# Router matmuls of two output stages with the router stationary and the tokens moving

## The chip, the cores and the metric

One core of a Trainium2 chip runs the whole kernel. The metric is the device time of one execution in microseconds, lower is better.

## What is computed

Two transformer blocks run one after the other on 1024 tokens of width 1024, in float32. Each block ends its mixer with an output projection and then sends the normed tokens to a mixture of experts, and it is the router in between that the change touches. Cut to that, the reference is:

```python
# first block, after the short-convolution mixer has given y
lat = lat + g1 * (y @ w_out)                        # output projection and residual
h = modulate(rms_norm(lat, norm_g), sh2, sc2)
aff = softmax(h @ w_router)                         # 16 router columns
g, idx = top_k(aff.T, 128)                          # each expert takes its best 128 tokens
# second block, after the mLSTM and pooling mixer
x = x + gate_a * (mix @ w_out)
h = rms_norm(x, norm2_g) * (1 + scale_f) + shift_f
g_logits = h @ w_rg + b_rg                          # 4 router columns
e_logits = h @ w_re + b_re                          # 32 more; kept together as 36 columns
# best group, best two experts in it, tokens sorted into blocks by expert
```

## The kernel before, in words

The program is written by hand, engine by engine. Each engine runs its own list of instructions in order, and the engines meet only at counting semaphores. Matrices are split into a high and a low part (type fp32r), and each product is made of three fp32r matmuls (helper `three`, L1719 to L1727); transposes and the router run in plain float32.

An **output stage** stands at the end of each block's mixer: `output_stage` exists once for each engine and runs twice, first with 16 router columns (`router1`), later with 36 (`router2`). It goes through the 1024 tokens in 8 tiles of 128. For tile t, TensorE multiplies the mixer's output with `w_out` into two PSUM banks (L1796 to L1806: eight chunks, two column halves, three fp32r matmuls each, 48 matmuls of 512 columns). VectorE then multiplies by the gate (L1268), adds the residual (L1271), ScalarE squares and sums (L893), VectorE and GpSimd make the inverse root (L1273, L634), and VectorE scales and shifts (L1276, L1279) into the one buffer `h2t`. GpSimd sends `h2t` to DRAM (L638), TensorE transposes it in eight pieces (L1788), ScalarE copies the transposed tile to `h2T` (L888), and TensorE multiplies it with the router (L1813).

The software pipeline is written out by hand. In step s, TensorE runs the projection of tile s, puts the eight transposes of tile s-1 in before chunk 6 of 8 (L1797), and the router of tile s-1 after chunk 8. The last step (s = 8) has no projection: transposes, then the router. ScalarE's step s is: slice and round the next tile of the mixer's output (L873), copy of `h2T` (L888), squares of tile s (L893). VectorE's L1268 writes `h2t` and so waits for three things: the projection of its tile (`y_ready`), the transposes of the tile before (`tr2`) and the landing of the tile before in DRAM (`h2_out`).

The router of a tile is 8 matmuls of depth 128: `h2T[:, k, :]` (128 columns, the tokens) is the stationary operand, `router[:, k, :]` (16 or 36 columns) moves. In the profile each float32 matmul has two records, so 8 matmuls are 16 passes. The logits of all tiles gather in PSUM bank 6, tokens on partitions, and VectorE reads them once at the end, in L1291 (first stage) and L1556 (second).

What follows the first stage on ScalarE: six DMA issues that bring back sums needed much later (L903), and the exponential of the softmax (L905), before which a table of functions is loaded. VectorE then picks the 128 best tokens for each expert in 16 rounds (L1304 to L1309), and everything after hangs on that. After the second stage VectorE works out ranks and slots (L1556 to L1625). SyncE starts to load expert weights into the ring of 12 buffers (L508, L550) as soon as its last residual tile of the stage is asked for.

TensorE, ScalarE and the others run the nine steps by `in_pairs` (L55): three steps written out, a hardware loop over pairs, the rest written out.

```python
                pe.wait_ge(S["h2T_ready" + b], s + past["h2T_ready" + b])
                for k in range(KD):
                    last = pe.matmul(ps[:, 6, bass.ds((s - 1) * width, width)], h2T[:, k, :], router[:, k, :],
                                     start=(k == 0), stop=(k == KD - 1))
                last.then_inc(S["rt_done" + b], 1)
```

Of the kernel before, what the change touches and what calls it, by code (L numbers as in the profile page):

```python
# [12 lines left out]
P = 128  # L13
D = 1024
T = 1024
NT = T // P
# [6 lines left out]
E1 = 16  # L23
# [9 lines left out]
    silu_ready sq_done mod_ready tr_ready tr_hi split_hi f_part cv_done c_copied route1 e1_exp m1_used m1_hi  # L33
    m1_xT m1_xT_hi slots_ready m1_silu m1_hT m1_hT_hi if_hi v_even gate_exp branch d2_out uc_ready cell_in
    q_mm m_mm dmask pm_ready m_out wt_diag wt_rest pv hn_tr num_out final_in dve_steps cols_tr mod_mm xn_done
    tr_lo sums_out sums2_out sums_in row_cols row_tr row_copied rows_out rows_here aff_ready affT_tr m1_xT_lo m1_hid m1_hT_lo if_lo v_odd if_mm gt_ready pool_mm k_mm k_out s_mm
    hn_ready q_out
"""

# [44 lines left out]
def build(nc, ctx, io, out, room):  # L84
# [23 lines left out]
    mod = sb("mod", [P, 2, 48])  # L108
    gain = sb("gain", [P, 4, 8])
    rowsT = sb("rowsT", [32, P])  # L110
    ident = sb("ident", [P, P])
    ones = sb("ones", [P, P])
    neghalf = sb("neghalf", [P, 8])
# [123 lines left out]
    for name in SEMS.split():  # L237
# [11 lines left out]
        [("row_tr", 1), ("row_tr_2", 1)],  # L249
        [("row_copied", 1), ("row_copied_2", 1)],  # L250
        [("rows_out", 16), ("rows_out_2", 16)],
        [("rows_here", 64), ("rows_here_2", 64)],
        [("var_ready", 1), ("var_ready_2", 1), ("hv_ready", 4)],
        [("rstd_ready", 1), ("rstd_ready_2", 1), ("hr_ready", 4)],
# [544 lines left out]
    def _(act):  # L799
# [67 lines left out]
        def output_stage(b):  # L867
            def token_slice(q, r):

                t = 2 * q + r  # L870
                if not (static(q) and t < 2):
                    act.wait_ge(S["y_ready" + b], t - 1 + past["y_ready" + b])
                act.activation(zsH[:, r, :, :], xz[:, :, bass.ds(t * P, P)], ACT.Copy).then_inc(S["zs_hi" + b], 1)  # L873

            token_slice(0, 0)
            for k in range(KD):
                if b == "":
                    split_hi(4, k, woH[:, k, :], (S["f_part"], 3 * KD) if k == 0 else None)
                else:
                    d2_hi(16 + k)  # L880

            def o_step(q, r):
                s = 2 * q + r
                if not (static(q) and s >= NT - 1):
                    token_slice(q, 1) if r == 0 else token_slice(q + 1, 0)
                if not (static(q) and s == 0):
                    act.wait_ge(S["tr2" + b], s + past["tr2" + b])
                    act.activation(h2T[:].rearrange("p (a b) c -> p a (b c)", a=2), ps[:, 4:6, :],  # L888
                                   ACT.Copy).then_inc(S["h2T_ready" + b], 1)
                if not (static(q) and s == NT):  # L890
                    act.wait_ge(S["x1_done" + b], s + 1 + past["x1_done" + b])

                    act.activation(h2t[:], xt[:, r, :], ACT.Square, accum_out=stat[:, 4, 0:1]).then_inc(S["sq2" + b], 1)  # L893

            in_pairs(act, NT + 1, o_step)
# [822 lines left out]
    def _(pe):  # L1718
# [61 lines left out]
        def output_stage(b, router, width):  # L1780
            def o_step(q, r):
                s = 2 * q + r
                first, final = static(q) and s == 0, static(q) and s == NT

                def transposes():
                    pe.wait_ge(S["h2_done" + b], s + past["h2_done" + b])
                    for c in range(KD):
                        last = pe.transpose(ps[:, 4 + c // 4, (c % 4) * P:(c % 4 + 1) * P], h2t[:, c * P:(c + 1) * P],  # L1788
                                            ident[:])
                    last.then_inc(S["tr2" + b], 1)  # L1790

                if not final:
                    pe.wait_ge(S["zs_lo" + b], s + 1 + past["zs_lo" + b])
                    if not (static(q) and s < 2):
                        pe.wait_ge(S["x1_done" + b], s - 1 + past["x1_done" + b])
                    for k in range(KD):  # L1796
                        if k == 6 and not first:  # L1797
                            transposes()
                        if first and b == "":
                            pe.wait_ge(S["split_done"], 3 * KD + k + 1)  # L1800
                        if first and b == "_2":
                            pe.wait_ge(S["d2_split"], 16 + k + 1 + past["d2_split"])
                        last = three([ps[:, 2 * r + n, :] for n in range(2)], zsH[:, r, k, :], zsL[:, r, k, :],
                                     [(woH[:, k, 512 * n:512 * n + 512], woL[:, k, 512 * n:512 * n + 512])
                                      for n in range(2)], k == 0, k == KD - 1)
                    last.then_inc(S["y_ready" + b], 1)  # L1806
                else:
                    transposes()
                if first:
                    return  # L1810
                pe.wait_ge(S["h2T_ready" + b], s + past["h2T_ready" + b])
                for k in range(KD):
                    last = pe.matmul(ps[:, 6, bass.ds((s - 1) * width, width)], h2T[:, k, :], router[:, k, :],  # L1813
                                     start=(k == 0), stop=(k == KD - 1))
                last.then_inc(S["rt_done" + b], 1)

            in_pairs(pe, NT + 1, o_step)

        pe.wait_ge(S["small_in"], 16 * 8)
        pe.wait_ge(S["row_copied"], 1)  # L1820
# [324 lines left out]
```

## Time and profile before

| | us |
|---|---|
| median of three runs | 2603.82 (2603.05 to 2608.44) |
| the profiled execution, its own time | 2599.45 |
| its span in the profile | 2597.8 |
| around the span | 1.65 |
| PE busy in the span | 2137.4 (82%) |
| first output stage, from PE's first projection matmul to the end of its last router matmul | 376.68 to 499.90 |
| second output stage, the same | 1612.57 to 1735.73 |

All times inside the execution are microseconds from the start of the span. PE is TensorE's matmuls and PEld its loads of stationary operands, DVE is VectorE, ACT ScalarE, POOL GpSimd, SP SyncE. A name with q behind it is an engine's instruction sequencer, which issues DMAs without the engine's arithmetic unit. In a row, `128*128 128x16` means a stationary operand of 128 rows by 128 columns and 16 moving columns. What stands in brackets is idle time and what ended it. A matmul's duration has its way through the array in it, so the pace of a run of them is read from start to start, not from durations.

### The profile page before, as it was taken

The numbers are of one execution on the slowest core, as the hardware profiler recorded it, in microseconds if no ns is written. First come the engines' busy times: TensorE is split into PE (matmuls) and PEld (weight loads), VectorE is DVE, ScalarE is ACT, GpSimd is POOL, SyncE is SP. The second block draws the span as 40 slices with busy tenths as digits, with TensorE's granted clock in tenths as the row PEclk, the third lists the DMA queues.
The fourth block names the chain that finished last, engine by engine and source line by source line (L and its number), as shares of the span: only waits on it lengthen the run. The fifth ranks groups of instructions, "written<-read, shape, count | busy, mean of one in ns | idle before, by whom it ended". The sixth has DMA issues, their size and how long they took to land. (4 is left out here: it accounts for less than half of the span.)

```text
span 2597.8 us, 30729 instructions
## 1 busy us (share of the span) xinstructions
PE 2137.4 (82%) x9605; PEld 1711.3 (66%) x9605; DVE 1711.3 (66%) x1868; ACT 1197.7 (46%) x1389; POOL 219.1 (8%) x261
## 2 busy tenths in 40 slices
PE   1899979729999999966989866963999999997850
PEld 1688868728888888855868445853888877775320
DVE  4566654589999999965053345444998989895015
ACT  2211112118777777753031323213888888884011
POOL 0000001000000000000000100103001101000013
PEclk9899989759999999996689977976999999998985
DMA  8077653519999999991010301343999999997645
GB/s 280 12 258 229 230 194 115 210 33 379 383 382 380 388 381 383 382 317 43 17 33 25 134 1 49 111 174 136 392 398 399 398 399 398 399 397 296 240 179 201
DMA packets 282879, 633.45 MB, mean 244 GB/s; under 512 B 24488, under 2 KB 63164, under 8 KB 282812
## 3 DMA queue, kind: packets, MB, share of 16 engines
q1 hardware_dynamic: 245248, 520.16, 54.7%
q0 software_dynamic: 27280, 97.10, 10.7%
q10 hardware_dynamic: 10284, 15.32, 1.7%
q8 instruction: 40, 0.66, 0.1%
q14 instruction: 27, 0.22, 0.0%
HBM read 573.18 MB, written 59.31 MB: 243 GB/s over the span
## 5 line engine op out<-in xcount | busy, mean ns | idle before, releaser
L1644 DVE TENSOR_TENSOR mL<-ring,mH 128x1024 fp32r<-128x1024 f32 x384 | 459.4, 1221 | 49.2 <-ACT mH L1057 40.3
L1324 DVE TENSOR_TENSOR mL<-ring,mH 128x1024 fp32r<-128x1024 f32 x384 | 459.1, 1223 | 33.2 <-ACT mH L911 14.4
L911 ACT ACTIVATE mH<-ring 128x1024 fp32r<-128x1024 f32 x384 | 403.3, 1061 | 95.9 <-PE ps L1726 95.8
L1057 ACT ACTIVATE mH<-ring 128x1024 fp32r<-128x1024 f32 x384 | 401.1, 1058 | 77.4 <-DMA ring<-in_w_expert_gate 30.5
L1723 PE MATMUL ps<-mH,xsH 128*128 128x512 f32 x1024 | 412.6, 403 | 7.3 <-DVE mL L1644 4.3
L1726 PE MATMUL ps<-mH,xsL 128*128 128x512 f32 x1024 | 402.0, 393 | 0.0
L1724 PE MATMUL ps<-mL,xsH 128*128 128x512 f32 x1024 | 401.1, 392 | 0.0
L1723 PEld LDWEIGHTS ps<-mH,xsH 128*128 128x128 f32 x1024 | 193.6, 189 | 46.1 <-issue 7.3
L1726 PEld LDWEIGHTS ps<-mH,xsL 128*128 128x128 f32 x1024 | 193.4, 189 | 43.0
L1724 PEld LDWEIGHTS ps<-mL,xsH 128*128 128x128 f32 x1024 | 193.9, 189 | 37.4
L1723 PE MATMUL ps<-mH,hidH 128*128 128x512 f32 x512 | 201.5, 394 | 3.5 <-DVE mL L1644 3.5
L1724 PE MATMUL ps<-mL,hidH 128*128 128x512 f32 x512 | 200.2, 391 | 0.0
L1726 PE MATMUL ps<-mH,hidL 128*128 128x512 f32 x512 | 158.2, 390 | 0.0
L1723 PE MATMUL ps<-hH,wH 128*128 128x512 f32 x384 | 151.7, 395 | 5.8 <-DVE wL L1183 5.8
L1724 PE MATMUL ps<-hL,wH 128*128 128x512 f32 x384 | 150.7, 392 | 0.0
L1144 DVE SCALAR_TENSOR_TENSOR acc<-ring,silu_c,acc 128x1024 f32<-128x1024 f32 x84 | 107.9, 1284 | 27.6 <-DMA ring<-in_ada_w 21.6
L1726 PE MATMUL ps<-hH,wL 128*128 128x512 f32 x384 | 119.1, 392 | 0.0
L1723 PE MATMUL ps<-woH,zsH 128*128 128x512 f32 x256 | 104.6, 408 | 11.2 <-DVE woL L1401 6.2
L1723 PEld LDWEIGHTS ps<-mH,hidH 128*128 128x128 f32 x512 | 96.5, 188 | 23.4 <-issue 3.7
L1726 PEld LDWEIGHTS ps<-mH,hidL 128*128 128x128 f32 x512 | 96.5, 189 | 20.4
L1724 PEld LDWEIGHTS ps<-mL,hidH 128*128 128x128 f32 x512 | 96.6, 189 | 19.5
L1724 PE MATMUL ps<-woL,zsH 128*128 128x512 f32 x256 | 101.8, 398 | 0.0
(357 smaller groups left out, 3147.2 us busy)
## 6 DMA issues: line engine op xcount, KB each, us to landing
ring<-in_w_expert_gate SPq DMA_DIRECT2D x144, 512.0 KB, 14.9
ring<-in_w_expert_up SPq DMA_DIRECT2D x144, 512.0 KB, 10.8
ring<-in_w_expert_down SPq DMA_DIRECT2D x144, 512.0 KB, 13.6
ring<-in_moe_w_gate SPq DMA_DIRECT2D x128, 512.0 KB, 8.3
ring<-in_moe_w_up SPq DMA_DIRECT2D x128, 512.0 KB, 7.7
ring<-in_moe_w_down SPq DMA_DIRECT2D x128, 512.0 KB, 8.0
ring<-in_ada_w SPq DMA_DIRECT2D x96, 512.0 KB, 5.4
yslot_dram<-xz POOLq DMA_DIRECT2D x32, 512.0 KB, 6.8
```

What stands on the lines that cost most here:

```text
L911: act.activation(mH[:, m % WSETS, :], ring[:, m % RING, :], ACT.Copy).then_inc(S["m1_hi"], 1)
L1057: act.activation(mH[:, wset, :], ring[:, slot, :], ACT.Copy).then_inc(S["m2_hi"], 1)
L1144: ins = dve.scalar_tensor_tensor(out=acc[:], in0=slot, scalar=silu_c[:, silu_col + k:silu_col + k + 1], in1=acc[:], op0=ALU.mult, op1=ALU.add)
L1324: dve.tensor_tensor(mL[:, m % WSETS, :], ring[:, m % RING, :], mH[:, m % WSETS, :].bitcast(F32), ALU.subtract).then_inc(S["m1_lo"], 1)
L1644: dve.tensor_tensor(mL[:, wset, :], ring[:, slot, :], mH[:, wset, :].bitcast(F32), ALU.subtract).then_inc(S["m2_lo"], 1)
L1723: pe.matmul(o, high, rh, start=start, stop=False)
L1724: pe.matmul(o, high, rl, start=False, stop=False)
L1726: last = pe.matmul(o, low, rh, start=False, stop=stop)
```

## The change

The operands of the router swap places: the router's 16 or 36 columns become stationary, and the tile's 128 tokens move. The result has logits on partitions and tokens along columns, in PSUM bank 7. ScalarE copies it to a new small buffer `lgT` in SBUF, and TensorE transposes it back into its place in bank 6, one step later and ahead of the next router, so that VectorE still reads the same layout. In the last step the last tile is transposed back at once. Two semaphores are added, `rl_done` (router matmuls done) and `lgT_copied`. ScalarE's copy stands between the copy of `h2T` and the squares. TensorE's nine steps are written out, without the hardware loop.

```diff
--- before.py
+++ after.py
@@ -33,7 +33,7 @@
     silu_ready sq_done mod_ready tr_ready tr_hi split_hi f_part cv_done c_copied route1 e1_exp m1_used m1_hi
     m1_xT m1_xT_hi slots_ready m1_silu m1_hT m1_hT_hi if_hi v_even gate_exp branch d2_out uc_ready cell_in
     q_mm m_mm dmask pm_ready m_out wt_diag wt_rest pv hn_tr num_out final_in dve_steps cols_tr mod_mm xn_done
-    tr_lo sums_out sums2_out sums_in row_cols row_tr row_copied rows_out rows_here aff_ready affT_tr m1_xT_lo m1_hid m1_hT_lo if_lo v_odd if_mm gt_ready pool_mm k_mm k_out s_mm
+    tr_lo sums_out sums2_out sums_in row_cols row_tr row_copied rows_out rows_here rl_done lgT_copied aff_ready affT_tr m1_xT_lo m1_hid m1_hT_lo if_lo v_odd if_mm gt_ready pool_mm k_mm k_out s_mm
     hn_ready q_out
 """
 
@@ -108,6 +108,7 @@
     mod = sb("mod", [P, 2, 48])
     gain = sb("gain", [P, 4, 8])
     rowsT = sb("rowsT", [32, P])
+    lgT = sb("lgT", [NR2, P])
     ident = sb("ident", [P, P])
     ones = sb("ones", [P, P])
     neghalf = sb("neghalf", [P, 8])
@@ -249,6 +250,8 @@
         [("row_tr", 1), ("row_tr_2", 1)],
         [("row_copied", 1), ("row_copied_2", 1)],
         [("rows_out", 16), ("rows_out_2", 16)],
+        [("rl_done", NT), ("rl_done_2", NT)],
+        [("lgT_copied", NT), ("lgT_copied_2", NT)],
         [("rows_here", 64), ("rows_here_2", 64)],
         [("var_ready", 1), ("var_ready_2", 1), ("hv_ready", 4)],
         [("rstd_ready", 1), ("rstd_ready_2", 1), ("hr_ready", 4)],
@@ -887,6 +890,11 @@
                     act.wait_ge(S["tr2" + b], s + past["tr2" + b])
                     act.activation(h2T[:].rearrange("p (a b) c -> p a (b c)", a=2), ps[:, 4:6, :],
                                    ACT.Copy).then_inc(S["h2T_ready" + b], 1)
+                    act.wait_ge(S["rl_done" + b], s + past["rl_done" + b])
+                    if not (static(q) and s == 1):
+                        act.wait_ge(S["rt_done" + b], s - 1 + past["rt_done" + b])
+                    width = E1 if b == "" else NR2
+                    act.activation(lgT[0:width, :], ps[0:width, 7, 0:P], ACT.Copy).then_inc(S["lgT_copied" + b], 1)
                 if not (static(q) and s == NT):
                     act.wait_ge(S["x1_done" + b], s + 1 + past["x1_done" + b])
 
@@ -1808,13 +1816,23 @@
                     transposes()
                 if first:
                     return
+                def token_logits(back):
+                    pe.wait_ge(S["lgT_copied" + b], s - back + 1 + past["lgT_copied" + b])
+                    pe.transpose(ps[:, 6, bass.ds((s - back) * width, width)], lgT[0:width, :],
+                                 ident[0:width, 0:width]).then_inc(S["rt_done" + b], 1)
+
+                if not (static(q) and s < 2):
+                    token_logits(2)
                 pe.wait_ge(S["h2T_ready" + b], s + past["h2T_ready" + b])
                 for k in range(KD):
-                    last = pe.matmul(ps[:, 6, bass.ds((s - 1) * width, width)], h2T[:, k, :], router[:, k, :],
+                    last = pe.matmul(ps[0:width, 7, 0:P], router[:, k, :], h2T[:, k, :],
                                      start=(k == 0), stop=(k == KD - 1))
-                last.then_inc(S["rt_done" + b], 1)
-
-            in_pairs(pe, NT + 1, o_step)
+                last.then_inc(S["rl_done" + b], 1)
+                if final:
+                    token_logits(1)
+
+            for s in range(NT + 1):
+                o_step(s // 2, s % 2)
 
         pe.wait_ge(S["small_in"], 16 * 8)
         pe.wait_ge(S["row_copied"], 1)
```

## Rows read from the trace of the kernel before

**Rows 1.** The page: busy time of each engine

```profile
PE 2137.4 (82%) x9605; PEld 1711.3 (66%) x9605; DVE 1711.3 (66%) x1868; ACT 1197.7 (46%) x1389; POOL 219.1 (8%) x261
```

**Rows 2.** Busy time by stretches, body and tail, first stage: PE PEld DVE ACT POOL PEclk DMA GB/s

```profile
394.00:484.00 90.00, 90.00 (x475) 76.65 (x474) 40.17 (x39) 19.89 (x27) 11.09 (x20) 1.00 0.50 171
484.00:505.00 21.00, 9.04 (x47) 7.48 (x46) 7.69 (x12) 3.76 (x5) 1.65 (x3) 0.59 0.72 264
```

**Rows 3.** Timeline of VectorE, gate multiply L1268: first stage, then second

```profile
404.57 1.23 DVE L1268 TENSOR_TENSOR h2t<-ps,gate_row 128x1024 f32<-128x1024 f32 x1 [5.90 <-DMA h_dram<-h2t]
...
456.86 1.22 DVE L1268 TENSOR_TENSOR h2t<-ps,gate_row 128x1024 f32<-128x1024 f32 x1 [4.66 <-DMA h_dram<-h2t]
...
486.02 1.23 DVE L1268 TENSOR_TENSOR h2t<-ps,gate_row 128x1024 f32<-128x1024 f32 x1 [7.16 <-DMA h_dram<-h2t]
...
1652.05 1.22 DVE L1268 TENSOR_TENSOR h2t<-ps,gate_row 128x1024 f32<-128x1024 f32 x1 [5.03 <-DMA h_dram<-h2t]
...
1692.60 1.23 DVE L1268 TENSOR_TENSOR h2t<-ps,gate_row 128x1024 f32<-128x1024 f32 x1 [5.43 <-PE ps L1726]
...
1707.52 1.23 DVE L1268 TENSOR_TENSOR h2t<-ps,gate_row 128x1024 f32<-128x1024 f32 x1 [6.70 <-DMA h_dram<-h2t]
1721.81 1.23 DVE L1268 TENSOR_TENSOR h2t<-ps,gate_row 128x1024 f32<-128x1024 f32 x1 [7.22 <-DMA h_dram<-h2t]
```

**Rows 4.** Timeline of TensorE around one router, at the full clock

```profile
401.94 1.85 PE L1813 MATMUL ps<-router,h2T 128*128 128x16 f32 x16
...
403.97 0.40 PE L1724 MATMUL ps<-woL,zsH 128*128 128x512 f32 x1
404.20 0.40 PE L1723 MATMUL ps<-woH,zsH 128*128 128x512 f32 x1
```

**Rows 5.** Timeline of TensorE: float32 matmuls of 256, then of 512 moving columns

```profile
1565.02 0.59 PE L1955 MATMUL ps<-qT,kT 128*128 128x256 f32 x2
...
1565.46 1.02 PE L1955 MATMUL ps<-qT,kT 128*128 128x512 f32 x2
```

**Rows 6.** The same timeline: small transposes after fp32r matmuls

```profile
1353.15 0.61 PE L1726 MATMUL ps<-gH,uL 128*128 128x512 f32 x2
1353.69 1.15 PE L1937 MATMUL ps<-ident,xz 4*128 4x4 f32 x16
```

**Rows 7.** Timeline, end of the first stage, TensorE, VectorE and ScalarE

```profile
496.31 3.59 PE L1813 MATMUL ps<-router,h2T 128*128 128x16 f32 x16 [1.11 <-ACT h2T L888]
...
499.94 0.29 DVE L1291 COPY lg<-ps 128x128 f32<-128x128 f32 x1 [6.77 <-PE ps L1813]
...
495.30 3.29 ACTq L903 DMA_DIRECT2D xz<-sums_dram  x6
498.62 1.28 ACT L905 ACT_TABLE_LOAD   x1 [2.36 <-issue]
500.91 0.31 ACT L905 ACTIVATE aff<-lg 128x128 f32<-128x128 f32 x1 [1.01 <-DVE lg L1297]
```

**Rows 8.** Timeline, end of the second stage

```profile
1732.10 3.63 PE L1813 MATMUL ps<-router,h2T 128*128 128x36 f32 x16 [1.11 <-ACT h2T L888]
1735.76 0.46 DVE L1556 TENSOR_TENSOR lg<-ps,bias 128x288 f32<-128x288 f32 x1 [6.80 <-PE ps L1813]
```

**Rows 9.** Nearest rows: ACT copy from PSUM, one narrow transpose, DMA issues

```profile
L1038 ACT ACTIVATE num<-ps x32: 278/278/281, 1494.9 to 1597.0; 128x129 f32<-128x129 f32 x32
...
566.33 0.28 PE L1831 MATMUL ps<-ident,top_v 16*128 16x16 f32 x1 [39.42 <-DVE top_f L1310]
...
1159.56 3.77 ACTq L946 DMA_DIRECT2D xz<-x_dram  x8
```

**Rows 10.** Timeline, tile 6 of the first stage: projection's end, router, squares

```profile
456.02 0.62 PE L1726 MATMUL ps<-woH,zsL 128*128 128x512 f32 x2
456.48 1.85 PE L1813 MATMUL ps<-router,h2T 128*128 128x16 f32 x16
...
459.37 1.06 ACT L893 ACTIVATE h2t<-xt 128x1024 f32<-128x1024 f32 x1 [4.41 <-DVE xt L1271]
```

## The prediction

> **What bounds the kernel now.** The page says that TensorE is busy for 82% of the span [rows 1], so one looks at TensorE first; but the change touches only the two output stages, and the share of the whole says nothing about them. The view by stretches shows that in the body of the first stage TensorE is busy without a gap at the full clock (90.00 of 90.00 us), and that in its tail the granted clock averages 0.59 and TensorE is busy for 9 of 21 us [rows 2]. Body and tail have to be priced apart.
>
> Is TensorE's work in the body also what sets the stage's end? The timeline of VectorE answers that. Its gate multiply L1268 opens the chain of every tile. In the first stage all seven after the first tile wait for the landing of `h2t` in DRAM, not for TensorE; three of them stand in the rows [rows 3]. In the second stage four wait for that landing too, the last two among them, and three in between for TensorE, 1692.60 the last of these [rows 3]. So the end of a stage hangs on the loop gate, squares, scale, DMA to DRAM, landing, gate. TensorE comes close: for tile 6 of the first stage the projection ends at 456.02 + 0.62 = 456.64, and VectorE starts at 456.86 [rows 3, 10]. A slower TensorE has about 0.2 us of room there and 1 us or more later; a faster one gives the first stage's body nothing.
>
> In the tails everything is serial: router, VectorE's read of the logits 0.04 us after it, routing, gather, experts [rows 7, 8]. What is added there moves the rest of the kernel.
>
> **The router itself, at the full clock.** Before, from the first router matmul (401.94) to the second fp32r matmul behind it (403.97) is 2.03 us; without a router the fp32r matmuls stand 0.23 apart, so a router costs 1.80 us, 0.112 a pass [rows 4]. With 16 columns moving, that is the price of loading 128 stationary columns. Afterwards the load is narrow and 128 columns move. The nearest row is float32 with 256 moving columns: two passes from 1565.02 to 1565.46, 0.22 each, so 0.110 for 128, if pace goes by columns [rows 5]. I take that: 16 x 0.110 = 1.76, a gain of 0.04 us a tile. The two limits, load of 128 and move of 128, happen to be the same size, and the change trades one for the other.
>
> The Trainium skill has a rule that reads otherwise. "TensorE: Matmul & The Clock Gate", section "Back-to-back issue gap", gives N/2.4 + 2.5 ns a matmul, an estimate of 56 ns for 128 columns; by it the router would fall to about 0.9 us a tile. The float32 row of 256 columns, 0.22 us, is twice what it gives, so the trace does not bear it out for this type. What it would do here is the third rival.
>
> **The transposes back** (one a tile from step 2 on). The nearest row is 16 transposes with 128 stationary and 4 moving columns in 1.15 us, under 0.07 each; before the first there is a gap of 1353.69 - 1353.15 - 2 x 0.23 = 0.08 us, with waits of its own in it [rows 6]. Bounds 0.03 and 0.15; I take 0.06, as all waits are over when TensorE gets there: `lgT` of the tile before was copied 12 us earlier. Net 0.02 us a tile slower. The first stage hides it; in the second, five tiles pass before the last one that TensorE releases, +0.1 us (bounds -0.2, +0.6).
>
> **ScalarE's copy in the body.** 0.28 us, by a copy of 129 columns from PSUM [rows 9]. It waits for the router and queued behind it are the squares of the next tile. The nearest approach is tile 6 of the first stage: the router ends at 458.33, the copy at 458.65, the squares start at 459.37 [rows 10]. 0.7 us remain, so nothing. The cover gone, each tile would pay what the copy overhangs.
>
> **The loop written out.** No gap between TensorE's steps in either form of step; in the body it is busy throughout [rows 2]. Nothing; bound 0 to 0.2 us for fetching more code.
>
> **Tail of the second stage.** At the half clock the router has 16 passes in 3.63 us [rows 8]; load of 128 against move of 128 is again equal (the first load gets shorter, the last move longer). Then come in series: hop to ScalarE 0.04, copy 0.28, hop to TensorE 0.05, one transpose 0.28 by the row of 128 stationary and 16 moving columns in a pause [rows 9], where before VectorE followed directly. +0.65 us, bounds 0.5 and 0.8. The transpose of tile 7 lies in the wait for `h2T` and costs nothing. GpSimd's constants wait for the same semaphore but are needed only 18 us later; so is ScalarE's exponential there, off the path.
>
> **Tail of the first stage.** The same 0.65 us would apply, but here ScalarE's queue decides. Before, ScalarE issued six DMAs (495.30, 3.29 us) and loaded the table (498.62, 1.28 us) while TensorE ran the last router; the exponential then only waited for VectorE and started at 500.91 [rows 7]. The new copy stands ahead of them in program order and waits for the router. So: router done 499.90, copy begins 499.94, issues begin 0.06 later, at 500.00 (the sequencer does not wait for the copy to end, as with the copy of `h2T` before). Six issues take 3.29 us as here, or 6/8 x 3.77 = 2.83 by the other run of such loads [rows 7, 9]. Then 0.03, and the table 1.28: 504.14 to 504.60. VectorE has the difference that the exponential reads 0.65 us later than before, at about 501.6, and waits. The exponential starts 3.2 to 3.7 us later than before; I take **+3.5 us**, nearer the row of the same six. Nothing takes this back: the ring of weights is full, and the 16 rounds of picking follow on VectorE. The sums land 5 us later too, but are used in TensorE's pause of 40 us before 566.33 [rows 9].
>
> **Sum.** First stage 0 + 3.5, second stage 0.1 + 0.65: +4.25 us, of which only 0.65 lies at a place that the change is about. Against the profiled execution, 2597.8 of span and 1.65 around it, that is 2599.45 + 4.25 = 2603.7. The median of the runs, 2603.82, lies 4.4 above that execution; the same addition gives **2608.1**. About 0.2% (5.2 us) is what a measurement of this kernel can tell from no change, so this forecast, +0.16%, lies just inside.
>
> **Rivals.**
>
> 1. *Slower: narrow load and move don't overlap.* If a pass pays its own narrow load before the move, it costs 0.112 x 16/128 = 0.014 us more in the first stage and 0.112 x 36/128 = 0.032 in the second. That is 0.5 us a tile in the second stage, five times on the path: +2.5; in the first, 5 x 0.2 less 0.2 of room, +0.8; half-clock tails, 16 x (0.028 + 0.063) = +1.5. Sum 4.25 + 4.8 = +9, 2612.9. Against it: today's passes do overlap load and move (0.112 for both together, where two passes of 256 columns with a full load keep 0.22). It turns the verdict once a pass costs some 0.007 us more.
>
> 2. *The hold of ScalarE's queue costs nothing*, since issues and table load get out while the copy waits. Then both tails pay 0.65: +1.4, 2605.2. Against it: ScalarE's instructions went in order everywhere here, and the issues started right behind L888's dispatch [rows 7].
>
> 3. *A float32 pass moves one column a cycle.* Price from rows: fp32r with 512 columns stands 0.23 apart, so 0.057 for 128 [rows 4]. A router saves 0.9 us. The first stage's body is bound by landings and gives nothing, the second's at most what separates 1692.60 from 1652.05 + 3 x 13.3 (the loop's period at its fastest, 404.57 to 456.86 in four tiles is 13.1), 0.6 to 1.2 us. The half-clock tails save 1.7 each. -0.9 - 3.4 + 4.25 = 0, 2603.8: even then not faster. It is the page's rule named above.
>
> 4. *The change doesn't do what it says*: the narrow load takes as long as a full one. Then a pass stays at 0.112, 0.04 us a tile more than forecast: +0.2, no other outcome.
>
> **How the numbers follow.** Forecast with rival 4 folded in 0.70, rival 1 0.12, rival 2 0.08, rival 3 0.05, none of them 0.05. The forecast's own bounds, 3.2 + 0.5 - 0.2 and 3.7 + 0.8 + 0.8, are +3.5 and +5.3, and three runs before spread by 5 us, so about a quarter of it counts as slower: 0.18 + 0.12 + 0.04 = 0.34. Faster needs a cause that I don't see: 0.04. Same 0.62. The range takes the forecast's bounds with a median's uncertainty of 1.5 us, rival 2 at the lower end and half of rival 1 at the upper: 2604.8 to 2612.0.
>
> **What would show it.** In the profile after: router passes 0.11 us from start to start in the body, 0.21 in the tails; `lgT` copies of 0.28 us; L1268 still released by landings in the first stage, its last one within 0.3 us of 486.02 and of 1721.81 in the second; the six sums' DMAs issued from 500.0 on, the table load at about 503; the exponential at 504.1 to 504.6; VectorE's read in the second stage 0.65 us later than 1735.76 plus what the first stage added. The prediction is wrong if the exponential starts before 502, if a pass in the body is below 0.09 or above 0.12, or if ScalarE's squares wait for a router.

## The result, and the profile after

The kernel after took 2613.33 us, median of 20 runs (2609.57 to 2619.38). The kernel before, run again beside it, took 2607.52 us in 20 runs (2599.46 to 2616.03). The ratio is 1.0024, 95% interval [1.0014, 1.0033]: 3.7 to 8.6 us slower. Ratios here and below compare fast runs alone, which leaves out one run of `unrolled` (3120.87 us, at a granted clock of 0.70). The forecast of +4.25 us (ratio 1.0016) lies inside the interval, but the predicted time, 2608.1, and its range up to 2612.0 do not hold the median. They stood on the three runs shown (2603.82), and the 20 runs of the same kernel lie 3.7 us higher. The rest of the miss is a step of the working, found below. The prediction gave "same" 0.62 and "slower" 0.34, with 0.2% as the least that can be told; the interval is clear of 1, and the 0.24% lies just above that mark.

The profiled execution after took 2610.95 us, its span 2609.3. Page, busy time of each engine, kernel after:

```profile
PE 2147.5 (82%) x9621; PEld 1709.6 (66%) x9621; DVE 1710.7 (66%) x1868; ACT 1202.1 (46%) x1405; POOL 217.6 (8%) x261
```

PE is busy for 10 us more than in [rows 1], with 16 more matmuls: the 16 transposes back. Cut at landmarks that both kernels have, the two spans (11.50 us apart) differ like this; each figure is the difference of two start times in the timelines:

| stretch | before | after | difference |
|---|---|---|---|
| start to the first projection matmul | 376.68 | 378.29 | +1.61 |
| stage 1, body: from there to the last copy of `h2T` | 118.55 | 121.58 | +3.03 |
| stage 1, tail: from there to the exponential | 5.68 | 9.05 | +3.37 |
| middle, up to the second stage's first projection matmul | 1111.66 | 1111.95 | +0.29 |
| stage 2, body | 118.45 | 121.17 | +2.72 |
| stage 2, tail: last copy of `h2T` to VectorE's read of the logits | 4.74 | 5.42 | +0.68 |
| the rest | 862.03 | 861.83 | -0.20 |

Both tails came as forecast (+3.5 and +0.65). Both bodies did not (0 and +0.1).

**The tails.** Timeline of TensorE, ScalarE and VectorE at the end of the first stage, kernel after:

```profile
499.76 0.28 PE L1821 MATMUL ps<-ident,lgT 16*128 16x16 f32 x1
499.87 1.02 ACT L891 ACTIVATE h2T<-ps 128x1024 f32<-128x1024 f32 x1 [5.47 <-PE ps L1796]
500.94 3.59 PE L1828 MATMUL ps<-h2T,router 128*16 128x128 f32 x16 [0.90 <-ACT h2T L891]
504.57 0.27 ACT L897 ACTIVATE lgT<-ps 16x128 f32<-16x128 f32 x1 [3.68 <-PE ps L1828]
504.63 2.96 ACTq L911 DMA_DIRECT2D xz<-sums_dram  x6
504.89 0.28 PE L1821 MATMUL ps<-ident,lgT 16*128 16x16 f32 x1 [0.36 <-ACT lgT L897]
505.22 0.29 DVE L1299 COPY lg<-ps 128x128 f32<-128x128 f32 x1 [7.41 <-PE ps L1821]
507.63 1.28 ACT L913 ACT_TABLE_LOAD   x1 [2.79 <-issue]
508.92 0.31 ACT L913 ACTIVATE aff<-lg 128x128 f32<-128x128 f32 x1
```

Against [rows 7] the router's own time is unchanged, 3.59 us for 16 passes. VectorE has the logits at 505.22, but the exponential starts at 508.92: the copy at 504.57 waited for the router, and behind it in ScalarE's order stand the six DMA issues (504.63 to 507.59) and the table load. In [rows 7] both ran beside the router. At the end of the second stage nothing stands in that place:

```profile
1743.12 3.63 PE L1828 MATMUL ps<-h2T,router 128*36 128x128 f32 x16 [0.86 <-ACT h2T L891]
1746.78 0.27 ACT L897 ACTIVATE lgT<-ps 36x128 f32<-36x128 f32 x1 [3.72 <-PE ps L1828]
1747.10 0.32 PE L1821 MATMUL ps<-ident,lgT 36*128 36x36 f32 x1 [0.36 <-ACT lgT L897]
1747.46 0.46 DVE L1564 TENSOR_TENSOR lg<-ps,bias 128x288 f32<-128x288 f32 x1 [7.47 <-PE ps L1821]
```

From the router's end at 1746.75 to VectorE's read there are 0.71 us where [rows 8] has 0.03.

**The body.** Timeline of TensorE around one transpose back and one router, second stage, kernel after:

```profile
1659.46 0.61 PE L1734 MATMUL ps<-woH,zsL 128*128 128x512 f32 x2
1660.00 0.25 PE L1821 MATMUL ps<-ident,lgT 36*128 36x36 f32 x1
1660.18 1.94 PE L1828 MATMUL ps<-h2T,router 128*36 128x128 f32 x16
1662.05 0.50 PE L1731 MATMUL ps<-woH,zsH 128*128 128x512 f32 x1
1662.38 0.40 PE L1732 MATMUL ps<-woL,zsH 128*128 128x512 f32 x1
```

and its loads of stationary operands:

```profile
1660.00 0.14 PEld L1821 LDWEIGHTS ps<-ident,lgT 36*128 36x128 f32 x1 [0.35 <-issue]
1660.18 1.67 PEld L1828 LDWEIGHTS ps<-h2T,router 128*36 128x36 f32 x16
1662.05 0.19 PEld L1731 LDWEIGHTS ps<-woH,zsH 128*128 128x128 f32 x1 [0.20 <-issue]
```

For comparison the same place in the kernel before:

```profile
1664.50 0.62 PE L1726 MATMUL ps<-woH,zsL 128*128 128x512 f32 x2
1664.73 1.98 PEld L1813 LDWEIGHTS ps<-router,h2T 128*128 128x128 f32 x16
1664.95 1.87 PE L1813 MATMUL ps<-router,h2T 128*128 128x36 f32 x16
1666.66 0.48 PE L1723 MATMUL ps<-woH,zsH 128*128 128x512 f32 x1
...
1666.97 0.39 PE L1724 MATMUL ps<-woL,zsH 128*128 128x512 f32 x1
```

Two things are to be seen. Before, the first load of the router starts at 1664.73, 0.22 us ahead of its matmul and beside the matmuls in flight. After, the loads of the transpose and of the first projection matmul (1662.05) start together with their own matmuls, behind gaps of 0.35 and 0.20 us that wait for nothing ("issue"). And the passes of the router are as forecast, 0.109 apart from the second one on (the first interval is 0.137), but from the last pair before the router (its first matmul) to the second matmul behind it there are 1662.38 - 1659.46 = 2.92 us. Before it is 2.47 (1664.50 to 1666.97). So this place costs 0.45 us more. Over the whole step of TensorE, from router to router, it is a little less: the step went from 13.63 to 14.01 us in the first stage and 14.04 in the second, 0.38 and 0.41 us a tile where I had 0.02.

Who then opens a tile? The timeline of VectorE, gate multiply, second stage, kernel after:

```profile
1702.43 1.23 DVE L1276 TENSOR_TENSOR h2t<-ps,gate_row 128x1024 f32<-128x1024 f32 x1 [5.83 <-PE ps L1734]
1717.13 1.23 DVE L1276 TENSOR_TENSOR h2t<-ps,gate_row 128x1024 f32<-128x1024 f32 x1 [6.49 <-DMA h_dram<-h2t]
1732.83 1.23 DVE L1276 TENSOR_TENSOR h2t<-ps,gate_row 128x1024 f32<-128x1024 f32 x1 [8.61 <-DMA h_dram<-h2t]
```

The last one that TensorE releases, 1702.43, stands 81.56 us behind the stage's first projection matmul, where 1692.60 [rows 3] stood 80.03 behind it: +1.53. The two intervals behind it are 14.70 and 15.70, where [rows 3] has 14.92 and 14.29: +1.19. Both of those end with a landing in DRAM while SyncE's loads of expert weights keep the DMA engines full (399 GB/s from 1722 to 1733). They did so before too (399 GB/s from 1711 to 1722), so full engines alone don't explain the difference.

### The profile page after: what moved, and what is told of

Read it like the earlier page. It is cut to its first block and busy times, and to the rows that moved or that the text cites. A ratio compares the mean times of both kernels' runs of the same rounds, so it can differ in the third digit from the quotient of the medians.

```text
span 2609.3 us, 30759 instructions
## 1 busy us (share of the span) xinstructions
PE 2147.5 (82%) x9621; PEld 1709.6 (66%) x9621; DVE 1710.7 (66%) x1868; ACT 1202.1 (46%) x1405; POOL 217.6 (8%) x261
```

## The experiments

**Theory A** after that comparison: each change of the stationary operand's shape (to 16 or 36 rows, to 16 or 36 columns, back to 128 by 128) costs TensorE about 0.09 us, because the load is then not run ahead of the matmuls in flight. **Rival:** the time is that of the 17 passes themselves, or of the waits put between them. For the tail of stage 1, A says that ScalarE's queue order costs 2.7 us of the 3.4; the rival, the serial copy and transpose.

**All shapes full** (`full_shape`). The router's stationary operand is read 128 columns wide, 16 or 36 of them meant and the rest spare (logits of no use, nobody reads them); the transpose back is 128 by 128.

```diff
-                    pe.transpose(ps[:, 6, bass.ds((s - back) * width, width)], lgT[0:width, :],
-                                 ident[0:width, 0:width]).then_inc(S["rt_done" + b], 1)
+                    pe.transpose(ps[:, 6, bass.ds((s - back) * width, P)], lgT[:], ident[:]).then_inc(S["rt_done" + b], 1)
...
-                    last = pe.matmul(ps[0:width, 7, 0:P], router[:, k, :], h2T[:, k, :],
+                    last = pe.matmul(ps[:, 7, 0:P], router[:, k * width:k * width + P], h2T[:, k, :],
```

**Only the transpose back full** (`rows_full`): the first of those two edits alone, with the spare rows of `lgT` set to zero; the router stays narrow.

> Of the changed kernel, with the router's stationary operand read 128 columns wide (the columns behind its own 16 or 36 give logits that nobody reads), and lgT transposed back as a full 128x128 tile. Theory A, array shape: TensorE's loads of stationary operands run ahead only between operands of the same rows and columns; each change of shape costs about 0.1 us, and the three changes in a tile (to the 16 or 36 rows of lgT, to the 16 or 36 columns of the router, back to 128x128) are the 0.4 us that a step grew (13.62 to 14.04 us). Then here the step is 13.62 + 0.11 for one full transpose = 13.73 us, the passes stand 0.112 apart, and no gap over 0.03 us stands around the back transpose. Theory B, waits: the added semaphore waits on TensorE stop the loading ahead, whatever the shapes; the step stays at 14.0 to 14.1. Theory C, the written-out loop: the same 14.0 to 14.1.

> Of the changed kernel, with lgT held as 128 rows, those behind the logits zero, and transposed back as a full tile; the router stays 16 or 36 columns wide. Theory A, array shape: the gap before the back transpose (0.09 us) goes and the 0.18 us from it to the router fall to about 0.11, while the change of columns after the router stays (0.20 and 0.33 us where 0.11 and 0.32 stood before the change): step 13.85 to 13.92 us. Theory B, waits, and theory C, the written-out loop: 14.0 to 14.1 us, with the gap before the back transpose in its place.

Timeline of TensorE around the router, second stage, `full_shape`:

```profile
1660.32 0.62 PE L1738 MATMUL ps<-woH,zsL 128*128 128x512 f32 x2
1660.78 0.27 PE L1825 MATMUL ps<-ident,lgT 128*128 128x128 f32 x1
1660.89 1.95 PE L1831 MATMUL ps<-h2T,router 128*128 128x128 f32 x16
1662.60 0.48 PE L1735 MATMUL ps<-woH,zsH 128*128 128x512 f32 x1
1662.91 0.40 PE L1736 MATMUL ps<-woL,zsH 128*128 128x512 f32 x1
```

and `rows_full`:

```profile
1661.60 0.62 PE L1735 MATMUL ps<-woH,zsL 128*128 128x512 f32 x2
1662.06 0.27 PE L1822 MATMUL ps<-ident,lgT 128*128 128x128 f32 x1
1662.26 1.94 PE L1828 MATMUL ps<-h2T,router 128*36 128x128 f32 x16
1664.13 0.50 PE L1732 MATMUL ps<-woH,zsH 128*128 128x512 f32 x1
1664.46 0.39 PE L1733 MATMUL ps<-woL,zsH 128*128 128x512 f32 x1
```

With full shapes the step is 13.69 us in the second stage, 0.06 more than before: the same instructions, waits and a bigger transpose, and yet 0.35 of the 0.41 us by which the change had lengthened it are gone. From pair to second matmul it is 2.59 us, and the transpose starts 0.46 behind the pair, without a gap. That ends the rival for the body. The runs do not show the gain: the ratios to the kernel before are 1.0031 [1.0015, 1.0046] for `full_shape` and 1.0035 [1.0021, 1.0048] for `rows_full`, against 1.0024 for the changed kernel, and what `full_shape` should save by its second body, 1.7 us, is less than two such medians tell apart. In `rows_full` the gap ahead of the transpose is gone too, but the one behind it is 0.20 instead of 0.11, and the way out of the router is as in the changed kernel; the step stays at 14.00 where A expected 13.85 to 13.92. A counted a switch into the transpose and another from it into the router; with the transpose full the first only moves to the router, and the longer transpose eats what is left (an account after the fact).

**Narrow router alone, without transposes between** (`late`). Each tile's transposed logits get their own place, and all eight transposes back run in the last step.

```diff
...
-                if not (static(q) and s < 2):
-                    token_logits(2)
+                if final:
+                    for t in range(NT - 1):
+                        token_logits(t)
...
```

> Of the changed kernel, with the copied logits of all tiles kept in an SBUF buffer of 16 or 36 rows by 1024, and all eight transposed back in the last step, seven of them while TensorE waits for the last h2T: the narrow router alone in the body. Theory A, changes of the array's shape at about 0.09 us each: two are left in a step, before and after the router, against 0.04 us that the 16 passes gain: step 13.75 to 13.80 us (13.62 before the change, 14.04 with it). Rival D: the cost sits in the back transpose itself and its wait; then the step is 13.58 us, and the narrow router pays for itself.

Timeline of TensorE around the router, second stage, `late`:

```profile
1661.08 0.61 PE L1732 MATMUL ps<-woH,zsL 128*128 128x512 f32 x2
1661.62 1.94 PE L1829 MATMUL ps<-h2T,router 128*36 128x128 f32 x16
1663.49 0.50 PE L1729 MATMUL ps<-woH,zsH 128*128 128x512 f32 x1
1663.83 0.40 PE L1730 MATMUL ps<-woL,zsH 128*128 128x512 f32 x1
```

The step is 13.85 and 13.91 us, above the expected 13.75 to 13.80. By the starts, entering costs 0.09 (0.54 us from the pair to the router, 0.45 before), the router and the way out of it 0.16 (1.87 to the next projection matmul, 1.71 before), and 0.03 follow up to the one after (0.34 against 0.31): 0.28, the whole of the step's difference in this stage. The 0.16 is 0.10 at the first interval between passes (0.136 against 0.032) and 0.09 behind the last pass (0.20 against 0.11), less 0.03 that the shorter passes gain. A has the cause, but its price of 0.09 a switch is too low. So the narrow router alone is slower than the one it replaces, 0.22 us a tile in the first stage and 0.28 in the second, though its passes are 0.003 us shorter. The transposes back add the rest: 0.16 and 0.13. The ratio is 1.0024 [1.0009, 1.0038].

Is it width as such? The kernel before has a place that says no. Its transposes of `gt` have a stationary operand 4 columns wide, and the large matmul follows the last of them without a gap (timeline of TensorE, kernel before):

```profile
1300.35 0.27 PE L1921 MATMUL ps<-ident,gt 128*4 128x128 f32 x1
1300.38 0.48 PE L1723 MATMUL ps<-gH,uH 128*128 128x512 f32 x1
```

There the load of 128 columns is run ahead of its matmul (by 0.03 us), and in all twelve profiles this distance is 0.03 or 0.07 us, where `late` has 0.20 behind the router's last pass. So theory A holds for the router's matmuls with 16 or 36 columns and for transposes with 16 or 36 rows, not for every narrow operand. Whether the number of columns or the kind of instruction (matmul or transpose) makes the difference was not tested.

**The order on ScalarE** (`act_order`). In the last step of the first stage the six DMA issues, and a dummy exponential that draws the table load, stand ahead of the copy of `lgT`.

```diff
...
+                    if static(q) and s == NT and b == "":
+                        act.wait_ge(S["zs_lo"], NT)
+                        act.wait_ge(S["sums_out"], 32)
+                        for part in range(6):
+                            act.dma_start(xz[:, 2 + part, :], sums_dram[part]).then_inc(S["sums_in"], 16)
+                        act.activation(spare[:], neghalf[:], ACT.Exp)
...
```

> Of the changed kernel, with the six DMA issues of the sums and a small exponential that loads the table put ahead of ScalarE's wait for the last router of the first stage. Theory: the hold of ScalarE's queue is worth 2.7 us of the first tail. From the start of the last copy of h2T to the softmax's exponential it was 5.68 us before the change and 9.05 after it; here 6.3 to 6.4, which leaves the 0.65 us of copy and transpose. The whole: 2.7 us faster than the changed kernel, 3 to 4 us slower than the kernel before. Rival: the exponential waits for something else too (the landing of sums, a clock at half speed), and stays over 8 us.

Timeline of ScalarE, end of the first stage, `act_order`:

```profile
497.59 1.02 ACT L892 ACTIVATE h2T<-ps 128x1024 f32<-128x1024 f32 x1 [5.47 <-PE ps L1799]
497.65 3.36 ACTq L898 DMA_DIRECT2D xz<-sums_dram  x6
501.04 1.28 ACT L899 ACT_TABLE_LOAD   x1 [2.43 <-issue]
502.33 0.21 ACT L899 ACTIVATE spare<-neghalf 128x8 f32<-128x8 f32 x1
502.45 0.25 ACT L904 ACTIVATE lgT<-ps 16x128 f32<-16x128 f32 x1
503.99 0.31 ACT L916 ACTIVATE aff<-lg 128x128 f32<-128x128 f32 x1 [1.29 <-DVE lg L1308]
```

From the copy of `h2T` to the exponential 6.40 us, against 9.05 in the changed kernel and 5.68 before: the hold of the queue is worth 2.65, the serial copy and transpose with hops the other 0.7. The body stayed at steps of 14.0. The ratio, 1.0030 [1.0015, 1.0045], shows no gain over the changed kernel's 1.0024; 2.65 us are less than what two such medians tell apart, so the saving rests on the trace alone.

**The loop written out, and nothing else** (`unrolled`: the kernel before, its nine steps of TensorE in a plain loop instead of `in_pairs`).

> The kernel before, with TensorE's nine steps of both output stages written out and nothing else. Theory A, array shape, says nothing of this: step 13.62 us, both stages start and end as before, whole within 0.1% of the kernel before. Theory C, the written-out loop: step 14.0 us, or up to 2 us more before the first stage (which starts 1.6 us later in the profile of the changed kernel), 3 to 6 us slower in all.

Ratio 1.0006 [0.9993, 1.0020], step 13.63, second body 118.56 against 118.45. Written-out code cost nothing that can be seen.

**Both repairs together** (`repaired`: `full_shape` with the order of `act_order`).

> Of the changed kernel, both repairs together: the router's stationary operand and lgT full 128x128, and the DMA issues and a small exponential ahead of ScalarE's wait for the last router of the first stage. By theory A and the queue theory: step 13.69 us, exponential 1.0 us after VectorE's read of the logits, and what is left is copy and transpose in two tails (0.65 us each) and about 0.4 us in the second body: 1.5 to 2 us slower than the kernel before. Rival: what the changed kernel lost in its runs (6 us) has another cause, and this one stays 5 us or more behind.

Ratio 1.0002 [0.9990, 1.0014], steps of 13.7, first tail 6.71, second 5.61 (full transposes and wider copies cost 0.2 to 0.3 in the half-clock tails). The expectation was 1.5 to 2 us behind the kernel before; the four stretches of this profile (119.30, 6.71, 119.61, 5.61) stand 3.8 us above those of `before`, and the interval reaches from 2.6 us faster to 3.7 slower. With both causes away no slowdown is left that the runs can tell, and no gain either. That each repair alone gives 1.0030 or 1.0031 and both together 1.0002 is more than the traces place (2.65 and 1.7 us), so part of that step is the scatter of medians.

**Without the landing wait** (`two_h2t`: the kernel before with two `h2t` buffers and a DMA semaphore for each).

```diff
-    h2t = sb("h2t", [P, D], scope=outp)
+    h2t = sb("h2t", [P, 2, D], scope=outp)
...
-                else:
-                    dve.wait_ge(S["tr2" + b], s + past["tr2" + b])
-                    dve.wait_ge(S["h2_out" + b], 16 * s + past["h2_out" + b])
+                elif not (static(q) and s < 2):
+                    dve.wait_ge(S["tr2" + b], s - 1 + past["tr2" + b])
+                    dve.wait_ge(h2o[r], 16 * q + XT_PAST[b])
```

**The change without the landing wait** (`two_change`: the changed kernel with both this and the order on ScalarE).

> The kernel before, with two buffers for h2t in turn, each with a DMA semaphore of its own, and without GpSimd's wait for the landing after each tile. Theory: the loop through the landing of h2t in DRAM sets the end of both output stages. Then every L1268 follows TensorE, its last one 2.1 us earlier than now (483.9 and 1719.7 where 486.0 and 1721.8 stand), TensorE's step stays at 13.62 us, and the whole is 3.5 to 4.5 us faster than the kernel before. Rival: the landing only hides another wait (the residual tile, GpSimd's power, the transposes), the last L1268 moves by less than 0.5 us, the whole stays within 1 us.

> The changed kernel with the two h2t buffers and two DMA semaphores (no wait for an h2t landing) and ScalarE's copy for the back transposes ahead of its DMA issues. Nothing but TensorE's own work paces the bodies now. Theory A (each change between the narrow and the full stationary costs TensorE about 0.09 us, 0.4 us a tile in all): step 14.0 in both stages against 13.64 and 13.61 of the kernel with two buffers, bodies 119.3 in both stages against 116.7 and 116.4, so 5.6 us more than that kernel with two buffers plus about 1.3 us of the two tails: about 2607, within 1 us of the kernel before. Rival (the 0.4 us a tile is a wait for a landing or for a buffer that the two buffers take away): step 13.65, bodies 116.5 and 117, total about 2602.

Timeline of VectorE, gate multiply, end of the second stage, `two_h2t`:

```profile
1694.15 1.23 DVE L1269 TENSOR_TENSOR h2t<-ps,gate_row 128x1024 f32<-128x1024 f32 x1 [5.42 <-PE ps L1727]
1707.76 1.23 DVE L1269 TENSOR_TENSOR h2t<-ps,gate_row 128x1024 f32<-128x1024 f32 x1 [5.39 <-PE ps L1727]
1721.20 1.22 DVE L1269 TENSOR_TENSOR h2t<-ps,gate_row 128x1024 f32<-128x1024 f32 x1 [6.37 <-PE ps L1727]
```

and `two_change`:

```profile
1698.18 1.23 DVE L1280 TENSOR_TENSOR h2t<-ps,gate_row 128x1024 f32<-128x1024 f32 x1 [5.84 <-PE ps L1738]
1712.22 1.23 DVE L1280 TENSOR_TENSOR h2t<-ps,gate_row 128x1024 f32<-128x1024 f32 x1 [5.83 <-PE ps L1738]
1726.08 1.22 DVE L1280 TENSOR_TENSOR h2t<-ps,gate_row 128x1024 f32<-128x1024 f32 x1 [6.78 <-PE ps L1738]
```

In both, TensorE now releases every tile, and its step is bare: 13.6 against 14.0. `two_h2t` takes 2600.90 us, the kernel before beside it 2607.36, ratio 0.9971 [0.9958, 0.9985]: it beats both kernels. Its bodies are 116.73 and 116.37, 1.8 and 2.1 us shorter than before: the 3.9 us are what was expected (3.5 to 4.5), and of the 6.5 us of the medians (interval 3.9 to 11.0) the trace places no more. `two_change` takes 2607.94, 1.0007 [0.9997, 1.0017]: by the difference of the two ratios (each to the kernel before beside it, on two different chips) the change costs that kernel 0.36%, some 9 us, with an uncertainty of some 4 us. The trace places 5.7 of it: from the first to the last copy of `h2T` +2.07 and +2.39, tails +0.59 and +0.68. I had expected bodies of 119.3, from seven steps; 117.55 and 118.79 were measured. The longer step enters six times, and in the first body the first copy also comes 1.25 us sooner after the first projection matmul (21.70 against 22.95), so that by the bodies of the table the sum is only 4.5. The rival, that the 0.4 us a tile is a wait for a landing or for a buffer, is gone with the landing wait.

**Both kernels once more** (`change_again`, `before_again`).

> The changed kernel once more, for how far one profile of it stands from the next. If the step and stage 2's body are the kernel's own: 14.0 and 121 us again, while the start of stage 1's projections and stage 1's body (a DMA's landing) may move by over 1 us. If they are a matter of the run: stage 2's body anywhere between 118.5 and 121.

> The kernel before once more. If the step and stage 2's body are the kernel's own: 13.62 and 118.5 us again, and stage 1's start within 376.7 to 380.4 as seen over the kernels so far. If not, both move.

Each is one execution: 2621.18 us the changed kernel, 2615.49 the kernel before, 5.7 apart and both well above their medians.

| | body 1 | tail 1 | body 2 | tail 2 | step 1, 2 |
|---|---|---|---|---|---|
| before | 118.55 | 5.68 | 118.45 | 4.74 | 13.63, 13.63 |
| before_again | 118.63 | 5.68 | 118.48 | 4.75 | 13.64, 13.63 |
| unrolled | 117.71 | 5.68 | 118.56 | 4.74 | 13.63, 13.63 |
| after | 121.58 | 9.05 | 121.17 | 5.42 | 14.01, 14.04 |
| change_again | 119.24 | 9.19 | 121.57 | 5.42 | 14.01, 14.04 |
| full_shape | 120.63 | 9.28 | 119.46 | 5.60 | 13.71, 13.69 |
| rows_full | 118.96 | 8.86 | 121.30 | 5.58 | 13.98, 14.00 |
| late | 118.60 | 8.96 | 120.13 | 5.39 | 13.85, 13.91 |
| act_order | 119.82 | 6.40 | 121.48 | 5.42 | 14.01, 14.05 |
| repaired | 119.30 | 6.71 | 119.61 | 5.61 | 13.73, 13.71 |
| two_h2t | 116.73 | 5.68 | 116.37 | 4.74 | 13.64, 13.63 |
| two_change | 117.55 | 6.27 | 118.79 | 5.42 | 14.01, 14.05 |

Tails, steps and the second body repeat to some tenths. Not so the first body of the changed kernel: 121.58 and 119.24. The 2.3 us between them belong to the execution, not to the change: 0.8 is there at the first gate multiply already (13.59 and 12.80 us behind the first projection matmul), and 1.5 is one landing (the sixth and seventh gate multiplies stand 16.59 and 15.08 us apart). The first of these moves the kernel before as well: 13.68 in `before`, 12.73 in `unrolled`, whose first body is 0.8 shorter. The starts of the first stage, 376.68 to 381.14 over all profiles, the stretch between the stages, 1111.7 to 1116.2, and the rest behind the second tail, 861.8 to 873.1, move as freely. What two profiles show of the change itself is therefore 0.6 to 3.0 in body 1, 3.4 to 3.5, 2.7 to 3.1 and 0.7: 7.4 to 10.3 us by the profiles, against 6.3 [3.7, 8.6] by the runs (1.0024 of 2607.5, with the interval's ends).

## Why the prediction was right and wrong

- **Router passes**: 0.110 forecast, 0.109 measured in the body; 3.59 and 3.63 us in the tails, unchanged. Right, as far as the pace of the passes goes. Rival 3 (one column a cycle) would have shown passes under 0.06; rival 1 (load and move in series) would have shown over 0.12 in the first stage and over 0.14 in the second. Both are out. That rival 1's 2612.9 is the number nearest to the 2613.33 measured is luck: its cost of 0.5 us a tile in the second stage was to sit in every pass, and the 0.41 measured sit at the edges.
- **"Net 0.02 us a tile slower": this step failed**, and with it first of all the router's term, 16 x 0.110 = 1.76, "a gain of 0.04 us a tile". Measured: 0.38 and 0.41 us a tile in all. By `late`, the narrow router alone costs 0.22 us a tile in the first stage and 0.28 in the second instead of gaining 0.04; the transposes back cost 0.16 and 0.13 where I had 0.06 with bounds 0.03 and 0.15. The old router I had measured with its edges, from its first matmul to the second projection matmul behind it (1.80); the new one I priced by the pace of its passes alone. By the same measure as the old one it takes 1.98 us in `late` (1663.83 - 1661.62 less 0.23), and starts 0.09 later behind the pair. So the switches into the router and back to the projection were put at nothing without a reason, and no bound carried them.
- A hint stood in [rows 6]: the gap of 0.08 us ahead of 16 transposes with a stationary operand of 4 rows. I put it down to the waits there, and my reason for going below it ("all waits are over") may have taken away the wrong thing. That the 0.08 is such a switch is not shown. A cleaner case stands in the kernel before, among float32 matmuls of 512 moving columns at the full clock: L1955 goes from 128 to 4 stationary rows at 1466.17, and the two intervals there are 0.52 and 0.53 us where the others are 0.43.
- The Trainium skill has a rule that may bear on this, and the prediction did not use it: "TensorEngine Tiling (Array Packing)", section "Key Properties", says that a change of tiling mode drains TensorE. The runs agree in sign: with every operand 128 by 128 the gaps are gone, with 36 rows or a router of 36 columns they are there. That the narrow operands here put the array into another mode is not shown by any run, so the mechanism stays open; what the runs show is the price of these shapes, and that the load isn't run ahead.
- **Body of the first stage, nothing: wrong, by 0.6 to 3.0.** The room of 0.2 us would have held a slowdown of 0.02 a tile. 0.4 us a tile used it up: in the changed kernel TensorE releases two gate multiplies of the first stage, 445.63 and 459.73 in the timeline, where before all seven wait for a landing (in `before_again` one of the seven, at 458.38, is TensorE's). I had named the room but not asked what the stage pays once it is gone. Counted from the first gate multiply, which leaves out how the stage started, the first body grew by 1.6 to 3.2.
- **Body of the second stage, +0.1, bounds -0.2 and +0.6: wrong, +2.7 and +3.1.** Half of it (1.5) is TensorE's step up to the last tile it releases. The other half (1.2 and 1.5) falls in the last two intervals, where landings decide, and this I did not foresee. `full_shape` shows some of it (intervals of 14.73 and 15.29), `late` ends at 15.34 and 14.33. With two buffers it is gone in both kernels. How the weight loads and this landing meet differently in the changed kernel was not settled.
- **ScalarE's copy in the body, nothing; the loop written out, nothing**: right. The copy reaches no square (behind the router of 459.61 the copy ends at 461.83, the squares start at 462.25 and had waited for VectorE), and `unrolled` is within its interval of 1.
- **Tail of the first stage, +3.5: right**, 3.37 (and 3.51 the second time), by the mechanism named: issues from 504.63, as the copy begins, then table, then exponential. The table load and the issues together are the 2.65 us that `act_order` got back. Rival 2 is out.
- **Tail of the second stage, +0.65: right**, 0.68.
- **Rival 4** (the narrow load takes as long as a full one, and a pass stays at 0.112) is out by the pace: 0.109 with the narrow operand, 0.112 in `full_shape`. It would have left the gaps out as well.

Two errors of different kinds thus stand in the absolute number: 3.7 us of the baseline, which three runs do not fix, and what the body lost by the switches, 3.3 to 6.1 us by the profiles where 0.1 was forecast, of which the medians show 1.6 (5.8 us between them against 4.25).

## What to carry to other kernels

Price a small matmul in the middle of large ones by what it does to the sequence, not by its own length: here the narrow router cost more on entering and leaving than two of its passes take, and spare columns in the operand were cheaper than narrow ones. Measure the new instruction with its edges, as the old one was measured. When an instruction that waits is put into an in-order queue, read what stands behind it: here six DMA issues and a table load lost their cover, nearly four times the price of the new work itself. And where an engine is busy throughout while another waits for a transfer, measure both loops: with the transfer's wait removed, the kernel before gained 6.5 us by the medians and 3.9 by the trace, which none of the kernels here that rewrote the router did.

## What the runs showed of the hardware that was not expected

- Between matmuls with a 128 by 128 stationary operand the load is run ahead (PEld 0.22 us ahead of its matmul). Around the router with 16 or 36 stationary columns, and before a transpose with 16 or 36 stationary rows, it starts with its own matmul. Around the 36-column router alone (`late`) the sequence loses 0.28 us: 0.09 up to its first pass, 0.19 from there to the second projection matmul behind it.
- Not every narrow operand does this: behind a transpose with 4 stationary columns the 128 by 128 matmul starts after 0.03 us, its load run ahead.
- A float32 pass with 36 stationary and 128 moving columns takes 0.109 us, one with 128 stationary and 36 moving 0.112, and one with 128 of both 0.112. This agrees with the longer of load and move setting the pace.
- Landings of the same 512 KB vary enough to move a stage that waits for them by 1.5 us from one execution to the next, while TensorE's step repeats to 0.01 us between two profiles of one kernel (13.63 and 13.64, 14.01 and 14.01, 14.04 and 14.04).
